# Attention probabilities scaled by GpSimd, and the copies of their transposes shared out anew

## The chip, the cores and the metric

The kernel runs on one core of a Trainium2 chip. Everything is fp32. The metric is the device time of one execution in microseconds (us), taken over whole executions of the program; the profile's span is the time from the first to the last instruction of one profiled execution.

The engines in this text: TensorE (PE; its weight loads are listed apart as PEld), VectorE (DVE), ScalarE (ACT), GpSimd (POOL) and SyncE (SP), which issues most of the loads. A "handoff" is the time between the end of an instruction on one engine and the start of the one that waited for it on another.

## The reference

Two transformer-like blocks of two layers each run over 256 tokens of width 1024. The first block is token mixing by three recurrences with SwiGLU layers, and it is the larger part of the time. The second block has an attention layer, which the change touches, then an HGRN layer, each followed by a SwiGLU layer. The attention:

```python
def gqa_attend(q, k, v):
    s = jnp.einsum('bkgqd,bksd->bkgqs', q, k, preferred_element_type=jnp.float32) * (HEAD_DIM ** -0.5)
    p = jax.nn.softmax(s, axis=-1).astype(v.dtype)
    return jnp.einsum('bkgqs,bksd->bkgqd', p, v)
...
    k_all = jnp.concatenate([k_c, k_l], axis=2)
    v_all = jnp.concatenate([v_c, v_l], axis=2)
    ...  # 256 latent queries, in blocks of 128, against all 512 keys
    o_c = gqa_attend(queries(h_ctx), k_c, v_c)   # 256 context queries against the 256 context keys
```

There are 16 query heads of width 64 and 4 key/value heads.

## The kernel before

The program is written out by hand, one instruction stream for each engine, with semaphores between them. No scheduler orders anything: each engine runs its list from top to bottom, and `wait_ge` holds it until a count is reached.

The attention works in 24 units (`attention_units`). A unit takes two heads (a pair `i`) at a time. The first 16 are **long units** (stream 0, `s == 0`): 128 latent queries against 512 keys, so two score tiles of 128x512. The last 8 are **short units** (stream 1): 256 context queries against 256 keys, so four score tiles of 128x256. Both kinds fill two PSUM banks with scores. For each unit `u`:

1. TensorE computes the scores into one of two pairs of banks (`scores`, `score_pair`).
2. VectorE takes the row maxima and makes the bias from them (`maxes`, L3709 and L3712).
3. ScalarE writes the exponentials into `Pb[:, u % 2]`, with the row sums as a by-product (`exps`, L3599).
4. VectorE inverts the sums (L3719) and multiplies the probabilities by them in place (`scale`, L3723); the last of these raises `probs_scaled`.
5. TensorE turns (transposes) the probabilities, eight tiles of 128x128, into the two banks of `turn_pair` (`turn_probs`, L463).
6. The two banks are copied to `PT` in SBUF (`keep_PT`; L3611 on ScalarE, L3731 on VectorE); each copy raises `PT_ready`. In long units ScalarE copies both banks, in short ones ScalarE copies the first and VectorE the second.
7. TensorE multiplies the values by the turned probabilities (`weigh`), and the result is copied out (`keep_o`; L3737 on VectorE for stream 0, L3618 on ScalarE for stream 1).

The units are pipelined by the loops that call these functions. In step `u` of its loop TensorE does `scores(u)`, `turn_probs(u - 2)` and `weigh(u - 3)`, in this order. `scores(u)` waits for `scores_read` of unit `u - 2`, and `turn_probs(v)` waits for `probs_scaled` of `v` and for both `PT_ready` of the unit before. VectorE does `maxes(u)`, `scale(u - 1)`, `keep_PT(u - 2)`, `keep_o`; ScalarE does `keep_PT(u - 2)`, `exps(u)`, `keep_o`. Recorded matmuls and loads stand at the lines of two helpers: L460 for products, L463 for turnings.

GpSimd has nothing to do in the attention. Its list goes from small loads ahead of it (L4612, L4614) to the wait for `lnp_free` and a load (L4616) long behind it.

Of the kernel before, what the change touches and what calls it, by code (L numbers as in the profile page):

```python
# [20 lines left out]
ALU = mybir.AluOpType  # L21
AX = mybir.AxisListType

P = 128
D = 1024
# [101 lines left out]
def two_blocks(nc, a, out):  # L127
    ctx = ExitStack()
    with ctx:
# [53 lines left out]
        expL_ready = sem("expL_ready")  # L183
        final_norm_landed = sem("final_norm_landed")
        forget_ready = sem("forget_ready")
# [36 lines left out]
        oT_ready = sem("oT_ready")  # L222
        out_norm_landed = sem("out_norm_landed")
        p_T_ready = sem("p_T_ready")
# [36 lines left out]
        std_ready = sem("std_ready")  # L261
        sw_ready = sem("sw_ready")
        v_tok_ready = sem("v_tok_ready")
        var_ready = sem("var_ready")
# [3273 lines left out]
        def act_attention(act):  # L3538
# [69 lines left out]
            def keep_PT(u):  # L3608
                for par in range(2 if units[u][1] == 0 else 1):
                    act.wait_ge(probs_turned, 2 * u + par + 1)  # L3610
                    ins = e.copy(PT[:, u % 4, par], turn_pair[:, par])  # L3611
                    ins.then_inc(act_step, act.up(act_step))
                    act.wait_ge(act_step, act.sent(act_step))
                    act.sem_inc(PT_ready, act.up(PT_ready))
# [7 lines left out]
            for u in range(len(units) + 4):  # L3622
                if 2 <= u < len(units) + 2:
                    keep_PT(u - 2)
                if u < len(units):
                    exps(u)
                if u >= 4 and units[u - 4][1]:
                    keep_o(units[u - 4][0])

        def dve_attention(dve):  # L3630
# [84 lines left out]

            def scale(u):
                r = by_query(u, am[:, 24:32])
                dve.wait_ge(probs_ready, dve.due(probs_ready))
                v.reciprocal(r, by_query(u, am[:, 8:16])).then_inc(dve_step, dve.up(dve_step))  # L3719
                dve.wait_ge(dve_step, dve.sent(dve_step))  # L3720
                n = 2 if units[u][1] == 0 else 4
                for j in range(n):
                    ins = v.tensor_scalar(probs(u, j), probs(u, j), r[:, j:j + 1], None, ALU.mult)  # L3723
                    done = probs_scaled if j == n - 1 else dve_step
                    ins.then_inc(done, dve.up(done))
                dve.wait_ge(dve_step, dve.sent(dve_step))
                dve.wait_ge(probs_scaled, dve.sent(probs_scaled))

            def keep_PT(u):
                dve.wait_ge(probs_turned, 2 * u + 2)  # L3730
                v.tensor_copy(PT[:, u % 4, 1], turn_pair[:, 1]).then_inc(dve_step, dve.up(dve_step))  # L3731
                dve.wait_ge(dve_step, dve.sent(dve_step))
                dve.sem_inc(PT_ready, dve.up(PT_ready))  # L3733

# [6 lines left out]
            for u in range(len(units) + 4):  # L3741
                if u < len(units):
                    maxes(u)
                if 1 <= u <= len(units):
                    scale(u - 1)
                if u >= 2 and u - 2 < len(units) and units[u - 2][1]:
                    keep_PT(u - 2)
                if u >= 4:
                    i, s, qt = units[u - 4]
                    if s == 0 and qt:  # L3750
                        keep_o(i)
# [682 lines left out]
        def pool_hgrn(pool):  # L4434
            e = pool.e
            pool.wait_ge(gb_ready, ends_out[-1])
            for back in range(2):
                pool.wait_ge(gE_ready, queries_exp[back])
                e.tensor_tensor(hF[back], hF[back], hq, ALU.mult).then_inc(pool_product, pool.up(pool_product))
            pool.wait_ge(out_norm_landed, pool.due(out_norm_landed, 16))  # L4440
            pool.wait_ge(hgrn_in_ready, gates_open[0])
# [106 lines left out]
        def second_dve(dve):  # L4548
# [10 lines left out]
            dve_x_sums(dve)  # L4559
            dve.wait_ge(final_norm_landed, dve.due(final_norm_landed, 16))  # L4560
            dve_ffn7(dve, ffn_gated_residual(dve, gtmp7, final=True),
# [15 lines left out]
        def pool_final_weights(pool):  # L4577

            pool.wait_ge(final_norm_landed, pool.due(final_norm_landed, 16))
            for tt in range(2):  # L4580
# [27 lines left out]
        def second_pool(pool):  # L4608
            e = pool.e
            pool.wait_ge(ln_used, pool.due(ln_used))  # L4610
            for j, n in enumerate(("attn_q_norm_2", "attn_k_norm_2")):
                e.dma_start(qkn[:, j], a[n][0:1, :].broadcast_to([P, 64])).then_inc(qk_norm_landed, 16)  # L4612
            pool.wait_ge(ln_cols_used, pool.due(ln_cols_used))
            e.dma_start(cst[:, LVL0:LVL0 + 3 * P], a["cst"][:, LVL0:LVL0 + 3 * P]).then_inc(lvl_landed, 16)  # L4614
            pool.wait_ge(lnp_free, pool.due(lnp_free))
            e.dma_start(lnp[:, 1], a["hgrn_out_norm_2"][0:1, :].broadcast_to([P, D])).then_inc(out_norm_landed, 16)  # L4616
            pool_hgrn(pool)
            e.dma_start(lnp[:, 1], a["final_norm_w_2"].rearrange("(a n) -> a n", a=1).broadcast_to([P, D])
                        ).then_inc(final_norm_landed, 16)
            pool_final_weights(pool)  # L4620
# [164 lines left out]
```

## Time and profile before

| | us |
|---|---|
| Time, median of 3 runs | 3075.56 |
| lowest and highest | 3074.17, 3078.39 |
| Profiled execution: its span | 3075.3 |
| PE busy | 2984.1 (97%) |
| PEld busy | 2376.8 (77%) |
| DVE busy | 1734.7 (56%) |
| ACT busy | 715.3 (23%) |
| POOL busy | 77.7 (3%) |

The profile gives no time for the profiled execution beside its span. The granted TensorE clock is full over the whole span (mean 0.998). Shares of the whole span say little about the change: the 24 attention units lie between about 1990 and 2076 us, less than 3% of the span, and in them VectorE and ScalarE are busy nearly as long as TensorE. A timeline row reads: start in us, duration in us, engine, line, operation, output and inputs, shape, number of instructions merged into the row, and in brackets the idle time of the engine just before, with what ended it.

### The profile page before, as it was taken

The page shows a single profiled execution, that of the slowest core. Times are in us where ns is not written, and L with a number is a line of the kernel's source. Part 1 is how long each engine was busy: PE and PEld are TensorE (multiplying, and loading weights), DVE is VectorE, ACT ScalarE, POOL GpSimd, SP SyncE. Part 2 cuts the span into 40 slices and gives each one's busy share as a digit, 9 for nine tenths or more (in the row PEclk, how much of TensorE's full clock was granted, in tenths as well). Part 3 has the DMA queues.
Part 4 walks back from the last instruction along what each step waited for, and adds up shares of the span by engine and source line. Part 5 has one row for each costly group of instructions (what it writes and reads, how often), then busy time and mean ns, then how long its engine had stood idle before and what let it go on. Part 6 is the DMA issues. An engine that isn't in the chain of part 4 may idle for free. (4 is left out here: it accounts for less than half of the span.)

```text
span 3075.3 us, 53460 instructions
## 1 busy us (share of the span) xinstructions
PE 2984.1 (97%) x23086; PEld 2376.8 (77%) x23086; DVE 1734.7 (56%) x2567; ACT 715.3 (23%) x1371; POOL 77.7 (3%) x105
## 2 busy tenths in 40 slices
PE   8999999999999999999999999989999999999998
PEld 8988775559987998685558985655888887766897
DVE  5554456446556564464546556584333664486666
ACT  2102114222112101223322104282111012254210
POOL 1000000000001000000000000000000000001000
PEclk9999999999999999999999999999999999999999
DMA  8645403237656746313227744102222443231553
GB/s 288 223 175 184 142 30 110 97 110 234 206 183 196 260 164 216 134 60 108 99 83 234 237 141 151 55 1 83 82 82 83 150 154 113 98 122 63 165 165 110
DMA packets 279818, 429.94 MB, mean 140 GB/s; under 512 B 10072, under 2 KB 147776, under 8 KB 279584
## 3 DMA queue, kind: packets, MB, share of 16 engines
q1 hardware_dynamic: 273936, 411.52, 39.5%
q0 software_dynamic: 5024, 13.82, 1.4%
q8 instruction: 183, 3.00, 0.4%
q10 hardware_dynamic: 624, 1.19, 0.1%
q14 instruction: 51, 0.42, 0.0%
HBM read 425.45 MB, written 1.05 MB: 139 GB/s over the span
## 5 line engine op out<-in xcount | busy, mean ns | idle before, releaser
L460 PE MATMUL bank<-arena 64*64 64x64 f32 (+8 forms) x7292 | 740.9, 281 | 23.3 <-DVE arena L2069 4.6
L460 PE MATMUL bank<-xT,ring 128*128 128x128 f32 (+2 forms) x4512 | 725.1, 320 | 10.3 <-DVE arena L852 5.7
L460 PEld LDWEIGHTS bank<-arena 128*128 128x128 f32 (+3 forms) x7292 | 640.6, 161 | 120.1 <-issue 36.6
L460 PEld LDWEIGHTS bank<-xT,ring 128*128 128x128 f32 (+1 forms) x4512 | 657.7, 191 | 71.2 <-issue 10.5
L460 PE MATMUL bank<-ring,xT 128*128 128x512 f32 (+3 forms) x1648 | 577.2, 519 | 2.2 <-DVEq L2086 1.2
L460 PEld LDWEIGHTS bank<-ring,xT 128*128 128x128 f32 (+1 forms) x1648 | 264.0, 182 | 253.5 <-issue 237.0
L460 PE MATMUL bank<-ring,arena 128*128 128x256 f32 (+1 forms) x1584 | 436.9, 427 | 12.4 <-issue 5.3
L460 PEld LDWEIGHTS bank<-ring,arena 128*128 128x128 f32 x1584 | 298.2, 190 | 123.9 <-issue 82.0
L852 DVE TENSOR_TENSOR arena<-arena,bank 128x256 f32<-128x256 f32 (+1 forms) x198 | 92.2, 466 | 395.7 <-PE bank L460 254.7
L763 ACT COPY arena<-bank 128x256 f32<-128x256 f32 (+1 forms) x264 | 107.7, 408 | 747.2 <-PE bank L460 745.9
L812 DVE TENSOR_TENSOR arena<-ring,arena 128x1024 f32<-128x1024 f32 (+1 forms) x216 | 257.1, 1190 | 7.4
L812 DVE TENSOR_TENSOR arena<-ring 128x1024 f32<-128x1024 f32 (+1 forms) x108 | 129.6, 1200 | 89.6 <-PE bank L460 84.7
L460 PE MATMUL bank<-arena,ring 128*128 128x128 f32 (+1 forms) x1152 | 168.2, 300 | 0.0
L460 PEld LDWEIGHTS bank<-arena,ring 128*128 128x128 f32 x1152 | 154.4, 192 | 7.0
L460 PE MATMUL bank<-xT,arena 128*128 128x128 f32 (+1 forms) x1104 | 157.9, 296 | 0.0
L460 PEld LDWEIGHTS bank<-xT,arena 128*128 128x128 f32 x1104 | 145.2, 192 | 5.8
L812 DVE TENSOR_TENSOR ring<-ring 128x1024 f32<-128x1024 f32 (+1 forms) x108 | 128.6, 1191 | 3.7
L463 PEld LDWEIGHTS bank<-cst,arena 128*128 128x128 f32 x482 | 54.0, 141 | 38.0 <-DVE arena L3723 22.2
L793 ACT COPY arena<-bank 128x256 f32<-128x256 f32 x14 | 5.2, 373 | 324.7 <-PE bank L460 324.7
L463 PE MATMUL bank<-cst,arena 128*128 128x128 f32 x482 | 66.9, 276 | 11.4 <-DVEq L3733 6.3
L906 DVE TENSOR_TENSOR arena<-arena,bank 128x256 f32<-128x256 f32 x56 | 23.6, 421 | 78.2 <-PE bank L460 77.1
L841 DVE TENSOR_TENSOR arena<-arena 128x512 f32<-128x512 f32 (+1 forms) x66 | 51.6, 781 | 25.6 <-ACT arena L782 21.1
(421 smaller groups left out, 2186.8 us busy)
## 6 DMA issues: line engine op xcount, KB each, us to landing
ring<-in_ffn_w SPq DMA_DIRECT2D x88, 1024.0 KB, 8.0
ring<-in_w_in SPq DMA_DIRECT2D x32, 2048.0 KB, 7.7
ring<-in_ffn_w_in SPq DMA_DIRECT2D x44, 1024.0 KB, 6.5
arena<-in_ada_w SPq DMA_DIRECT2D x20, 2048.0 KB, 13.2
ring<-in_ffn_w SPq DMA_DIRECT2D x16, 2048.0 KB, 7.9
ring<-in_ffn_w_out SPq DMA_DIRECT2D x12, 2048.0 KB, 7.8
ring<-in_hgrn_w_in SPq DMA_DIRECT2D x12, 2048.0 KB, 7.9
ring<-in_ffn_w SPq DMA_DIRECT2D x8, 1536.0 KB, 6.6
```

Source lines behind the costliest of these rows:

```text
L460: return self.e.matmul(o, lhsT, rhs, start=start, stop=stop, skip_group_check=True)
L463: return self.e.transpose(o, x, ident[0:n, 0:n])
L763: ins = e.copy(w.s[:, i], bank[:, 0:w.T])
L793: e.copy(w.kept[:, 0], banks[0][:, 0:256]).then_inc(down_kept, act.up(down_kept))
L812: v.tensor_tensor(out_, a_, b_, ALU.subtract).then_inc(T_sums, dve.up(T_sums))
L841: ins = v.tensor_tensor(w.hid_block(b), c4[:, :, :, 0], c4[:, :, :, 1], ALU.mult)
L852: ins = v.tensor_tensor(out_, kept, c, ALU.add)
L906: v.tensor_tensor(out_, a_, b_, ALU.add).then_inc(done, dve.up(done))
```

## The change

It does three things in the attention, and one that only renames.

- The inversion of the row sums stays on VectorE, in a function `invert`, and raises a new semaphore, `sums_inverted`. The multiplications go to GpSimd, in a new function `pool_attention`, called between the two loads named above. It has one wait for `sums_inverted` per unit and a wait for its own completion behind each of its multiplications: 32 of 128x512 and 32 of 128x256.
- In long units ScalarE copies the first bank of the turned probabilities and VectorE the second.
- In short units VectorE copies both, and ScalarE none.
- `final_norm_landed` and `out_norm_landed` become one semaphore, `lnp_row_landed`, with counts 16 and 32.

```diff
@@ act_attention
             def keep_PT(u):
-                for par in range(2 if units[u][1] == 0 else 1):
-                    act.wait_ge(probs_turned, 2 * u + par + 1)
-                    ins = e.copy(PT[:, u % 4, par], turn_pair[:, par])
+                if units[u][1] == 0:
+                    act.wait_ge(probs_turned, 2 * u + 1)
+                    ins = e.copy(PT[:, u % 4, 0], turn_pair[:, 0])
                     ins.then_inc(act_step, act.up(act_step))
                     act.wait_ge(act_step, act.sent(act_step))
                     act.sem_inc(PT_ready, act.up(PT_ready))
@@
+        def pool_attention(pool):
+            e = pool.e
+            for u in range(len(attention_units())):
+                r = by_query(u, am[:, 24:32])
+                pool.wait_ge(sums_inverted, u + 1)
+                n = 2 if units_stream(u) == 0 else 4
+                for j in range(n):
+                    ins = e.tensor_scalar(probs(u, j), probs(u, j), r[:, j:j + 1], None, ALU.mult)
+                    done = probs_scaled if j == n - 1 else pool_step
+                    ins.then_inc(done, pool.up(done))
+                    pool.wait_ge(done, pool.sent(done))
@@ dve_attention
-            def scale(u):
-                r = by_query(u, am[:, 24:32])
+            def invert(u):
                 dve.wait_ge(probs_ready, dve.due(probs_ready))
-                v.reciprocal(r, by_query(u, am[:, 8:16])).then_inc(dve_step, dve.up(dve_step))
-                dve.wait_ge(dve_step, dve.sent(dve_step))
-                n = 2 if units[u][1] == 0 else 4
-                for j in range(n):
-                    ins = v.tensor_scalar(probs(u, j), probs(u, j), r[:, j:j + 1], None, ALU.mult)
-                    done = probs_scaled if j == n - 1 else dve_step
-                    ins.then_inc(done, dve.up(done))
-                dve.wait_ge(dve_step, dve.sent(dve_step))
-                dve.wait_ge(probs_scaled, dve.sent(probs_scaled))
+                ins = v.reciprocal(by_query(u, am[:, 24:32]), by_query(u, am[:, 8:16]))
+                ins.then_inc(sums_inverted, dve.up(sums_inverted))
+                dve.wait_ge(sums_inverted, dve.sent(sums_inverted))
 
             def keep_PT(u):
-                dve.wait_ge(probs_turned, 2 * u + 2)
-                v.tensor_copy(PT[:, u % 4, 1], turn_pair[:, 1]).then_inc(dve_step, dve.up(dve_step))
-                dve.wait_ge(dve_step, dve.sent(dve_step))
-                dve.sem_inc(PT_ready, dve.up(PT_ready))
+                for par in (1,) if units[u][1] == 0 else range(2):
+                    dve.wait_ge(probs_turned, 2 * u + par + 1)
+                    v.tensor_copy(PT[:, u % 4, par], turn_pair[:, par]).then_inc(dve_step, dve.up(dve_step))
+                    dve.wait_ge(dve_step, dve.sent(dve_step))
+                    dve.sem_inc(PT_ready, dve.up(PT_ready))
@@ loop of dve_attention
                 if 1 <= u <= len(units):
-                    scale(u - 1)
-                if u >= 2 and u - 2 < len(units) and units[u - 2][1]:
+                    invert(u - 1)
+                if 2 <= u < len(units) + 2:
                     keep_PT(u - 2)
@@ second_pool
+            pool_attention(pool)
             pool.wait_ge(lnp_free, pool.due(lnp_free))
```

On VectorE, two long units in a row of the program before (`bank` is PSUM, `arena` is SBUF; L3723 is the scaling, L3737 the copy of a finished head pair):

```order
L3709 TENSOR_REDUCE arena<-bank 128x2
L3712 TENSOR_SCALAR arena<-arena 128x2
L3719 RECIPROCAL arena<-arena 128x2
L3723 TENSOR_SCALAR arena<-arena 128x512 x2
L3709 TENSOR_REDUCE arena<-bank 128x2
L3712 TENSOR_SCALAR arena<-arena 128x2
L3719 RECIPROCAL arena<-arena 128x2
L3723 TENSOR_SCALAR arena<-arena 128x512 x2
L3737 COPY arena<-bank 128x256
```

The same place of the changed program (its lines stand some 11 lower; here L3737 is the copy of a turned bank and L3743 that of a finished pair):

```order
L3721 TENSOR_REDUCE arena<-bank 128x2
L3724 TENSOR_SCALAR arena<-arena 128x2
L3730 RECIPROCAL arena<-arena 128x2
L3737 COPY arena<-bank 128x512
L3721 TENSOR_REDUCE arena<-bank 128x2
L3724 TENSOR_SCALAR arena<-arena 128x2
L3730 RECIPROCAL arena<-arena 128x2
L3737 COPY arena<-bank 128x512
L3743 COPY arena<-bank 128x256
```

Two scalings from SBUF have gone from each long unit, and one copy from PSUM has come.

On VectorE, two short units in a row before:

```order
L3709 TENSOR_REDUCE arena<-bank 128x4
L3712 TENSOR_SCALAR arena<-arena 128x4
L3719 RECIPROCAL arena<-arena 128x4
L3723 TENSOR_SCALAR arena<-arena 128x256 x4
L3731 COPY arena<-bank 128x512
L3709 TENSOR_REDUCE arena<-bank 128x4
L3712 TENSOR_SCALAR arena<-arena 128x4
L3719 RECIPROCAL arena<-arena 128x4
L3723 TENSOR_SCALAR arena<-arena 128x256 x4
L3731 COPY arena<-bank 128x512
```

And now:

```order
L3721 TENSOR_REDUCE arena<-bank 128x4
L3724 TENSOR_SCALAR arena<-arena 128x4
L3730 RECIPROCAL arena<-arena 128x4
L3737 COPY arena<-bank 128x512 x2
L3721 TENSOR_REDUCE arena<-bank 128x4
L3724 TENSOR_SCALAR arena<-arena 128x4
L3730 RECIPROCAL arena<-arena 128x4
L3737 COPY arena<-bank 128x512 x2
```

Four scalings have gone from each short unit, and a second copy has come. TensorE's list is the same before and now.

## Rows read from the trace of the kernel before

**Rows 1.** Busy time by engine, turnings 2 to 9, seven units (PE, PEld, DVE, ACT, POOL).
```profile
2000.88:2022.62 21.74, 21.74 (x198) 14.07 (x196) 18.38 (x38) 18.55 (x42) 0.00 (x0) 1.00 0.01 2
```

**Rows 2.** Timeline, one long unit on TensorE and VectorE.
```profile
2014.33 2.15 PE L460 MATMUL bank<-arena 128*64 128x128 f32 x20
...
2016.62 1.22 DVE L3709 TENSOR_REDUCE arena<-bank 128x2 f32<-128x1024 f32 x1 [0.57 <-PE bank L460]
...
2018.29 0.88 DVE L3723 TENSOR_SCALAR arena<-arena 128x512 f32<-128x512 f32 x2
...
2019.52 1.09 PE L463 MATMUL bank<-cst,arena 128*128 128x128 f32 x8
```

**Rows 3.** Timeline, the first exponential of two long units on ScalarE.
```profile
2009.88 0.69 ACT L3599 ACTIVATE arena<-bank,arena 128x512 f32<-128x512 f32 x1 [0.20 <-ACT arena L3611]
...
2013.07 0.69 ACT L3599 ACTIVATE arena<-bank,arena 128x512 f32<-128x512 f32 x1 [0.20 <-ACT arena L3611]
```

**Rows 4.** Timeline of TensorE, turnings 1 and 15.
```profile
1997.77 1.09 PE L463 MATMUL bank<-cst,arena 128*128 128x128 f32 x8 [0.67 <-DVE arena L3723]
...
2041.74 1.07 PE L463 MATMUL bank<-cst,arena 128*128 128x128 f32 x8
```

**Rows 5.** Timeline, one short unit on VectorE and TensorE.
```profile
2062.19 1.23 DVE L3709 TENSOR_REDUCE arena<-bank 128x4 f32<-128x1024 f32 x1
2062.25 1.06 PE L463 MATMUL bank<-cst,arena 128*128 128x128 f32 x8 [0.60 <-DVEq L3733]
...
2063.24 2.15 PE L460 MATMUL bank<-arena 128*64 128x256 f32 x16
...
2063.87 1.14 DVE L3723 TENSOR_SCALAR arena<-arena 128x256 f32<-128x256 f32 x4
...
2065.10 0.69 DVE L3731 COPY arena<-bank 128x512 f32<-128x512 f32 x1
...
2065.94 1.23 DVE L3709 TENSOR_REDUCE arena<-bank 128x4 f32<-128x1024 f32 x1
```

**Rows 6.** Timeline, the last turnings (22 and 23) and the last copy.
```profile
2069.74 1.06 PE L463 MATMUL bank<-cst,arena 128*128 128x128 f32 x8 [1.67 <-DVEq L3733]
...
2072.28 1.06 PE L463 MATMUL bank<-cst,arena 128*128 128x128 f32 x8 [0.46 <-DVEq L3733]
...
2073.39 0.69 DVE L3731 COPY arena<-bank 128x512 f32<-128x512 f32 x1 [1.31 <-PE bank L463]
```

**Rows 7.** Timeline, GpSimd beside VectorE and ScalarE in the first block.
```profile
517.25 2.53 DVE L2387 TENSOR_TENSOR arena<-arena 128x256 f32<-128x256 f32 x4
...
519.86 1.10 POOL L2327 TENSOR_TENSOR arena<-arena 128x512 f32<-128x512 f32 x1 [0.36 <-DVE arena L2387]
...
521.05 0.42 ACT L2300 ACTIVATE arena<-arena 128x256 f32<-128x256 f32 x1 [0.59 <-POOL arena L2327]
...
581.28 1.27 POOL L2545 TENSOR_TENSOR arena<-arena 128x512 f32<-128x512 f32 x1 [56.54 <-ACT arena L2575]
582.62 2.27 POOL L2545 TENSOR_TENSOR arena<-arena,cst 128x512 f32<-128x512 f32 x2
```

**Rows 8.** Timeline of GpSimd, its other kinds and sizes.
```profile
0.24 0.10 POOL L4776 MEMSET const-float32-0.0<- 128x1 f32 x1 [0.24 <-issue]
...
31.46 0.20 POOL L1217 MEMSET rows<- 128x128 f32 x1 [10.16 <-ACTq L3132]
...
2808.53 4.67 POOL L4445 TENSOR_TENSOR xT<-xT,lnp 128x1024 f32<-128x1024 f32 x2 [10.12 <-ACTq L4238]
...
3031.71 1.26 POOL L4583 TENSOR_TENSOR xtok<-xtok,lnp 128x512 f32<-128x512 f32 x1 [217.64 <-DVEq L3352]
```

**Rows 9.** Timeline of VectorE around GpSimd's last row above.
```profile
3029.35 0.69 DVE L3339 TENSOR_TENSOR arena<-arena,lnp 128x512 f32<-128x512 f32 x1
...
3031.64 0.42 DVE L906 TENSOR_TENSOR arena<-arena,bank 128x256 f32<-128x256 f32 x1
3032.10 1.42 DVE L3339 TENSOR_TENSOR arena<-arena,lnp 128x512 f32<-128x512 f32 x1
```

More of the change, by code:

```diff
@@ L183, in two_blocks @@
         expL_ready = sem("expL_ready")
-        final_norm_landed = sem("final_norm_landed")
         forget_ready = sem("forget_ready")
@@ L222, in two_blocks @@
         oT_ready = sem("oT_ready")
-        out_norm_landed = sem("out_norm_landed")
+        lnp_row_landed = sem("lnp_row_landed")
         p_T_ready = sem("p_T_ready")
@@ L262, in two_blocks @@
         sw_ready = sem("sw_ready")
+        sums_inverted = sem("sums_inverted")
         v_tok_ready = sem("v_tok_ready")
@@ L4439, in pool_hgrn @@
                 e.tensor_tensor(hF[back], hF[back], hq, ALU.mult).then_inc(pool_product, pool.up(pool_product))
-            pool.wait_ge(out_norm_landed, pool.due(out_norm_landed, 16))
+            pool.wait_ge(lnp_row_landed, pool.due(lnp_row_landed, 16))
             pool.wait_ge(hgrn_in_ready, gates_open[0])
@@ L4559, in second_dve @@
             dve_x_sums(dve)
-            dve.wait_ge(final_norm_landed, dve.due(final_norm_landed, 16))
+            dve.wait_ge(lnp_row_landed, dve.due(lnp_row_landed, 32))
             dve_ffn7(dve, ffn_gated_residual(dve, gtmp7, final=True),
@@ L4577, in pool_final_weights @@
         def pool_final_weights(pool):
-            pool.wait_ge(final_norm_landed, pool.due(final_norm_landed, 16))
+            pool.wait_ge(lnp_row_landed, pool.due(lnp_row_landed, 16))
             for tt in range(2):
@@ L4614, in second_pool @@
             e.dma_start(cst[:, LVL0:LVL0 + 3 * P], a["cst"][:, LVL0:LVL0 + 3 * P]).then_inc(lvl_landed, 16)
+            pool_attention(pool)
             pool.wait_ge(lnp_free, pool.due(lnp_free))
-            e.dma_start(lnp[:, 1], a["hgrn_out_norm_2"][0:1, :].broadcast_to([P, D])).then_inc(out_norm_landed, 16)
+            e.dma_start(lnp[:, 1], a["hgrn_out_norm_2"][0:1, :].broadcast_to([P, D])).then_inc(lnp_row_landed, 16)
             pool_hgrn(pool)
             e.dma_start(lnp[:, 1], a["final_norm_w_2"].rearrange("(a n) -> a n", a=1).broadcast_to([P, D])
-                        ).then_inc(final_norm_landed, 16)
+                        ).then_inc(lnp_row_landed, 16)
             pool_final_weights(pool)
```

## Prediction

> **What bounds the kernel now.** I read the page first: TensorE is busy for 97% of the span at full clock. So a change on other engines can cost time wherever TensorE waits for them, and can win only what TensorE waits for now. Then I read the timeline of the attention, where alone the change acts, and followed one unit through the engines.
>
> In long units TensorE works without a pause at first: seven units take 21.74 us, and it is busy for 21.74 of them [rows 1]. That is 3.106 us per unit, and no change on other engines makes it less. ScalarE, with both copies, needs 3.19 (2009.88 to 2013.07) [rows 3] and falls behind, until later TensorE follows its pace. The 14 steps from turning 1 to turning 15 take 43.97 us [rows 4] where TensorE alone would need 43.48. So only 0.5 us can be won there.
>
> In short units VectorE is the bound: from one maximum to the next 3.75 us pass (2062.19 to 2065.94), filled by maximum, bias and inverse, 1.68 until the scaling starts, then four scalings in 1.14 and a copy that with its gap takes 0.84 (2065.10 to 2065.94). TensorE needs only 0.99 (the turning, 2062.25 to 2063.24) + 2.15 = 3.14 [rows 5]. From turning 15 to turning 22 the 7 steps take 28.00 us, 4.00 each, as ScalarE's backlog falls into the first of them [rows 4, 6].
>
> **The change, part by part.** Let p be the time of one GpSimd scaling of 128x512, and q that of one of 128x256. Neither is in the trace.
>
> *The loop that the change makes longer.* The scaling used to lie on VectorE between the inverse and the turning. Now it lies there on GpSimd. In step u TensorE does the scores of u, turns u-2, weighs u-3. VectorE inverts unit u-1 behind the maximum of u, and GpSimd can start on u-1 only then. So there is a ring: scores of u, maximum of u, inverse of u-1, GpSimd on u-1, turning of u-1 (in step u+1), weighing, scores of u+2. It spans two units; each microsecond by which it is too long costs half a microsecond per unit.
>
> *Long units.* The inverse ends at 2018.26 (0.03 before the scaling at 2018.29), the turning of this unit starts at 2019.52 [rows 2]: a window of 1.26 us. Before, the scaling filled 0.88 of it. Now it must hold a handoff from VectorE to GpSimd (0.08: 517.25 + 2.53 = 519.78, start 519.86), two scalings, the wait for its own completion between them (0.07: two of 1.10 in 2.27) and a handoff on (0.09: 520.96 to 521.05) [rows 7]; handoff to TensorE taken as that to ScalarE. The turning is late by d = 2p + 0.24 - 1.26 = 2p - 1.02, if that is positive. Over 14 steps: 43.48 + 7d - 43.97 = 14p - 7.63.
>
> *Short units.* The same ring, for two units: TensorE's end to VectorE's start 0.14 (2016.48 to 2016.62 [rows 2]), maximum to end of inverse 1.65, GpSimd 0.08 + 4q + 3 x 0.07 + 0.09 = 4q + 0.38, turning 0.99, weighing and scores 2.15 [rows 5]. Sum 5.31 + 4q. Over 7 steps: 3.5 x (5.31 + 4q) - 28.00 = 14q - 9.42. VectorE's own work is now 1.68 + 2 x 0.84 = 3.36 per unit, a floor of the step; it binds while q is below 0.35.
>
> *Off the path.* ScalarE loses 24 copies. In long units it had 3.19 of work against TensorE's 3.106 and loses one of two copies; in short ones VectorE set the step, and ScalarE loses its only copy. So it is late in neither; its backlog at turning 15 goes, and that gain is in the 28.00 above. VectorE's copy in long units (0.84) takes the place of scalings (0.88), so its load stays. The wait in `keep_PT` holds the next maximum behind it on VectorE; the bank is half turned by then and the copy starts within the turning, so the ring above stays the longer one. GpSimd's list has only the wait for `lnp_free`, hundreds of microseconds later, behind the new work: nothing. The renamed semaphore: nothing.
>
> *End.* The last short unit has two copies in a row on VectorE. Before, the copy starts at 2073.39; now the second starts after half a turning (0.53), 0.05 and 0.84: 2073.70, 0.3 late [rows 6]. For GpSimd's longer work before turning 23 I allow another 0.2 (an estimate). Together +0.5.
>
> *Sum:* 14p - 7.63 + 14q - 9.42 + 0.5 = 14 (p + q) - 16.55.
>
> **The two unknown prices.** From below: a MEMSET only writes, 0.10 us for one element per partition and 0.20 for 128 [rows 8], so 0.8 ns per element, and p = 0.50, q = 0.30. From above: a TENSOR_TENSOR reads two tensors and writes one, 1.26 us for 512 and 4.67 / 2 = 2.34 for 1024 [rows 8], so 2.1 ns per element, and p = 1.26, q = 0.72. A scaling reads one and writes one. It has one stream more than the first and one less than the second, so I take the middle: p = 0.88, q = 0.51. Then the sum is 14 x 1.39 - 16.55 = +2.9 us: long units +4.7 (half of 2p - 1.02 = 0.74 in each, 3.48 per step), short units -2.3 (3.67 per step), end +0.5. On the profiled span, 3075.3 + 2.9 = 3078.2; the median of the runs is 0.3 above that span, so 3078.5.
>
> Two ops of GpSimd of 512 elements show 1.26 and 1.10 us here [rows 7, 8], and no single-input one is in the trace. The Trainium skill, GPSIMD Engine Reference, section Elementwise — side-by-side cycle accounting, gives a measured 769 ns for 512 elements as its best case. An estimate from that page is p = 0.77 and q = 0.38, by which the sum would be 14 x 1.15 - 16.55 = -0.4, so 3075.1; it would still be no change that can be told.
>
> **The rivals.**
>
> *GpSimd is fast (p near 0.50).* For it: a scaling need not share its reads with a second tensor, and MEMSET goes at 0.8 ns. Against it: reads and writes may share time as the two reads seem to. Then d is nothing, the long part is -0.5, and short steps are held by VectorE's 3.36: 7 x 3.36 - 28.00 = -4.5. With the end +0.5: -4.5, or 3071.1. Even that is less than 0.2%.
>
> *GpSimd is as slow as with two inputs (p = 1.26, q = 0.72).* This is the one on the other side. Place: the same ring, each second turning waits 1.5 us. Price 14 x 1.98 - 16.55 = +11.2, or 3086.8. It counts as slower (by over 0.2%, 6.2 us, about what a measurement of this kernel can tell from no change) from p + q = 1.62, which on the line between the two bounds is p = 1.03. For it: the arithmetic of GpSimd in these rows runs near that rate. Against it: all of it has two inputs.
>
> *VectorE and GpSimd hold each other up.* The trace shows it: beside GpSimd's TENSOR_TENSOR (3031.71 to 3032.97), VectorE's operation with two inputs in SBUF took 1.42 us where the same took 0.69 before. But an operation that had one of its inputs in PSUM, and was running when GpSimd started, took its usual 0.42 [rows 9]. In the attention VectorE's long operations (maximum, copies) read PSUM alone, so I cost this at nothing. If the copies of the turned banks, which start just behind the inverse and so beside GpSimd, were held for one scaling each, VectorE would need 1.68 + 0.84 + 0.88 = 3.40 in a long unit, still under 3.48, but 3.36 + 2 x 0.51 = 4.38 in a short one against 3.67 (+5.0 over 7). With the sum above +7.9: 3083.5.
> The Trainium skill, SBUF — State Buffer, section Who interferes with whom, says that VectorE in a two-port mode and GpSimd block each other for a whole instruction, and that a VectorE instruction with at most one SBUF input outside these modes does not contend. The pair of rows on the two VectorE operations agrees; the large SBUF scaling that could contend leaves VectorE with this change, and what is left (bias and inverse, 2 or 4 elements) comes behind two copies and a maximum (0.84 + 0.84 + 1.23 = 2.91 in a short unit), when GpSimd's work on a unit (4q + 0.21 = 2.25) is done.
>
> **How the numbers follow.** Forecast (p between 0.65 and 1.03): 0.54. Fast GpSimd: 0.15. Slow GpSimd (p above 1.03): 0.25. Mutual blocking: 0.06. The first gives -2 to +6, which is within 0.2%; so does nearly all of the second. Faster by over 0.2% needs -6.2 us, more than the sum of all floors wins: 0.03, for what I have overlooked. Slower: of the last two cases nearly all, 0.29, less a little for the part of them that stays under the bound: 0.28. Same: 0.69. The range goes from the fast case, 3071.5, to the slow one at its full price, 3087; beyond them I leave about 0.15 together.
>
> **What would show it.** GpSimd scalings of about 0.88 and 0.51 us. Turnings in long units alternate: one step near 3.1, the next near 3.85, with TensorE waiting for GpSimd in each second step. Short steps near 3.7, where TensorE waits for GpSimd too, and VectorE idles a little. No wait of TensorE for ScalarE's exponentials at the change from long to short. VectorE's copies at 0.69 though GpSimd runs beside them. I am wrong if TensorE waits for something other than GpSimd in most steps, if maxima or copies are longer than before, or if GpSimd's gaps are much over 0.1 us.

## The result, and the profile after

| | before | changed |
|---|---|---|
| Time, median of 6 runs (us) | 3076.36 | 3102.57 |
| lowest and highest | 3073.87, 3078.39 | 3100.80, 3121.43 |
| ratio of the times | | 1.0096, 95% interval 1.0086 to 1.0106 |
| Span of the profiled execution | 3075.3 | 3100.5 |
| POOL busy | 77.7 | 157.1 |

By the medians the change costs 26 us (0.85%). The ratio of 0.96% comes out higher, since the one execution of 3121.43 counts in it; its mean granted clock was 0.990, that of the others 0.995 to 0.997. Either way the time lies clearly outside the predicted range of 3071.5 to 3087. The profiled execution's own time was 3102.53. The forecast was a small loss of 2.9 us; a loss it is, but nine times as large.

All of it arises in the attention. The page shows the engines over 40 slices of the span; look at slice 27 of DVE, ACT and POOL. The kernel before:

```profile
DVE  5554456446556564464546556584333664486666
ACT  2102114222112101223322104282111012254210
POOL 1000000000001000000000000000000000001000
```

The changed kernel:

```profile
PE   8999999999999999999999999979999999999998
DVE  5554556446646555455446556554433564486666
ACT  2102114221112102213221113352111011255210
POOL 1000000000001000000000000270000000001000
```

TensorE's first product of attention scores began at 1989.10 before and begins at 1985.58 in this execution; the first product behind the attention began at 2075.88 and begins at 2101.24. So the attention takes 115.66 us in place of 86.78, 28.9 more. The 3.5 us by which it begins earlier are not the change's doing: over all the kernels of this text that have the attention, whose programs ahead of it differ by a small instruction or two at most, it begins between 1985.58 and 1991.13. What comes behind takes as long as it did (999.4 and 999.3 us).

One long unit in the timeline of the changed kernel (L3637 is GpSimd's scaling):

```profile
2041.08 1.09 PE L463 MATMUL bank<-cst,arena 128*128 128x128 f32 x8 [0.63 <-POOL arena L3637]
2042.10 2.15 PE L460 MATMUL bank<-arena 128*64 128x128 f32 x20
...
2042.29 3.22 POOL L3637 TENSOR_SCALAR arena<-arena 128x512 f32<-128x512 f32 x2 [1.27 <-DVE arena L3730]
...
2044.37 1.22 DVE L3721 TENSOR_REDUCE arena<-bank 128x2 f32<-128x1024 f32 x1 [0.83 <-PE bank L460]
2045.57 1.09 PE L463 MATMUL bank<-cst,arena 128*128 128x128 f32 x8 [1.31 <-POOL arena L3637]
...
2045.83 0.17 DVE L3730 RECIPROCAL arena<-arena 128x2 f32<-128x2 f32 x1
2046.16 3.23 POOL L3637 TENSOR_SCALAR arena<-arena 128x512 f32<-128x512 f32 x2 [0.65 <-DVE arena L3730]
...
2049.44 1.09 PE L463 MATMUL bank<-cst,arena 128*128 128x128 f32 x8 [0.70 <-POOL arena L3637]
```

This answers to [rows 2]. There the window from the inverse to the turning was 1.26 us; here two scalings alone take 3.22, and each turning waits for GpSimd, which ends at 2045.51 and 2049.39. TensorE waits for VectorE only once more, for 0.23 us at the last weighing. Its waits for GpSimd in the attention, in the changed kernel (total us, times, longest):

```profile
PE bank L463 <- POOL arena L3637: 28.5, 20, 3.8
```

The prices, from the groups of instructions between 1990 and 2101 us (count, busy us, mean ns):

```profile
L3637 POOL TENSOR_SCALAR arena<-arena 128x512 f32<-128x512 f32 x32 | 50.0, 1563 | 104.3 <-DVE arena L3730 102.6
...
L3637 POOL TENSOR_SCALAR arena<-arena 128x256 f32<-128x256 f32 x32 | 29.5, 922 | 9.9 <-DVE arena L3730 7.4
L3737 DVE COPY arena<-bank 128x512 f32<-128x512 f32 x32 | 22.1, 692 | 20.2 <-PE bank L463 18.5
```

So p = 1.56 and q = 0.92, where the prediction took 0.88 and 0.51 and held 1.26 and 0.72 for the upper ends. VectorE's copies stay at 0.69 us.

There is a second thing that the prediction did not have: TensorE's clock. Its two levels are 1.2 GHz, shown as 0.50, and 2.4 GHz, shown as 1.00. Busy time and granted clock by stretches in the changed kernel (PE, PEld, DVE, ACT, POOL, then the clock):

```profile
1995.00:1997.00 2.00, 2.00 (x8) 0.76 (x6) 0.69 (x1) 1.70 (x4) 1.85 (x2) 0.50 0.00 0
1997.00:2003.00 6.00, 3.99 (x34) 2.46 (x33) 3.81 (x7) 2.42 (x7) 3.53 (x3) 0.99 0.00 0
2003.00:2007.20 4.20, 4.20 (x26) 2.20 (x24) 0.69 (x1) 2.14 (x5) 2.72 (x2) 0.61 0.00 0
2007.20:2035.00 27.80, 21.39 (x196) 14.06 (x196) 17.67 (x32) 14.21 (x33) 19.75 (x13) 1.00 0.01 2
...
2071.00:2076.60 5.60, 4.62 (x24) 2.88 (x24) 2.47 (x5) 2.56 (x9) 4.61 (x5) 0.70 0.01 3
2076.60:2082.00 5.40, 3.26 (x26) 2.03 (x24) 4.54 (x8) 2.70 (x10) 3.10 (x4) 1.00 0.00 2
2082.00:2087.00 5.00, 4.36 (x24) 3.03 (x24) 1.38 (x2) 2.20 (x8) 4.28 (x5) 0.66 0.01 2
```

From 1995 to 1997 it is at the lower level, and again for parts of later stretches, behind longer waits of TensorE: it had waited 2.18 us before the turning at 1993.68, and 2.78 before that at 2082.64. Such a turning takes 1.97 us where [rows 2] has 1.09. Not every long wait brings it: TensorE also waited 1.97 us before the turning at 2012.39, and the stretch around it is at 1.00. For the whole attention, from its first product to the first one behind it, before and then changed:

```profile
1989.10:2075.88 86.78, 77.98 (x665) 51.40 (x665) 70.04 (x154) 70.93 (x179) 0.00 (x0) 1.00 0.00 1
```
```profile
1985.58:2101.24 115.66, 86.39 (x665) 55.77 (x665) 63.99 (x114) 56.78 (x155) 79.52 (x64) 0.93 0.00 1
```

The same 665 products and turnings keep TensorE busy for 8.4 us longer.

### The profile page after: what moved, and what is told of

It is laid out like the page before. It is cut to its first block, busy times and chain, and to the rows that moved or that the text cites. A ratio compares the mean times of both kernels' runs of the same rounds, so it can differ in the third digit from the quotient of the medians.

```text
span 3100.5 us, 53484 instructions
## 1 busy us (share of the span) xinstructions
PE 2988.7 (96%) x23086; PEld 2381.2 (77%) x23086; DVE 1728.3 (56%) x2527; ACT 700.7 (23%) x1347; POOL 157.1 (5%) x169
## 4 chain that ended last, share of the span: by engine, by line
PE 88%; DVE 7%; ACT 2%; POOL 1%; issue 1%; DMA 0%; DVEq 0%; ACTq 0%; POOLq 0%
PE bank L460 86%; PE bank L463 2%; POOL arena L3637 1%; DVE arena L812 1%; DVE arena L3721 1%; DVE ring L812 0%; ACT xT L1086 0%; DVE arena L906 0%; DVE arena L2069 0%; DMA xtok<-in_x 0%; DVE arena L2081 0%; DVE arena L4409 0%; DVE stats L1001 0%; DVE xT L1108 0%; DVE arena L1903 0%
## 5 line engine op out<-in xcount | busy, mean ns | idle before, releaser
L3637 POOL TENSOR_SCALAR arena<-arena 128x512 f32<-128x512 f32 (+1 forms) x64 | 79.5, 1242 | 114.3 <-DVE arena L3730 110.0
```

Of the source, the lines that this page charges most:

```text
L3637: ins = e.tensor_scalar(probs(u, j), probs(u, j), r[:, j:j + 1], None, ALU.mult)
```

## The experiments

The theory (A): GpSimd's own price, put into the ring between the inverse and the turning, makes the time; each microsecond there costs half a microsecond per unit. Rivals: VectorE beside it makes GpSimd slow (B in e1); the new sharing of the copies costs (B in e2 and e3); the clock adds to it (C) or not (D). To compare stages closely I use one length throughout, from turning 1 to the first product behind the attention, each from its own profile: 78.11 us before (1997.77 to 2075.88), 103.87 changed (1997.37 to 2101.24). I call it the stage. It leaves out the head of the attention, from the first product of scores to turning 1, which takes 8.67 us before and 11.79 changed; where that matters it is said.

**e1: GpSimd's operations alone.** A small kernel of its own, all work of the original left out.

```python
run(lambda: e.tensor_scalar(y[:, 0:w_], y[:, 0:w_], s[:, 0:1], None, ALU.mult))     # L48
run(lambda: e.tensor_scalar(y[:, 0:w_], y[:, 0:w_], 0.5, None, ALU.mult))           # L49
run(lambda: e.tensor_tensor(y[:, 0:w_], y[:, 0:w_], w[:, 0:w_], ALU.mult))          # L50
run(lambda: e.tensor_tensor(y[:, 0:w_], y[:, 0:w_], s[:, 0:1].broadcast_to([P, w_]), ALU.mult))  # L51
```

> This kernel leaves the whole computation out: it only times GpSimd. Sets of four, each waiting for its own completion: multiplication by a per-partition scalar from SBUF, by a constant, by a second tensor, by a broadcast column, at 512 and 256 elements; the first at 1024, and one tensor_tensor of 2x512 by two broadcast columns; then the scaling of 512 beside VectorE maxima out of PSUM, and beside VectorE copies out of PSUM and tiny SBUF scalings. Theory A (the price is GpSimd's own): the scaling of 512 takes 1.5 to 1.6 us with VectorE idle too, 256 takes 0.92, and beside maxima it is the same. Rival B (VectorE beside it makes it slow): 0.6 to 1.1 us alone and 1.5 beside the maxima. The broadcast form of 1024 should take 2.3 by the rows of tensor_tensor, against 2 x 1.56.

Groups of its instructions (L60 and L61 are the scaling of 512 with VectorE busy beside it, L53 the broadcast form of 2x512):

```profile
L60 POOL TENSOR_SCALAR y<-y,s 128x512 f32<-128x512 f32 x8 | 12.5, 1565 | 1.0 <-POOL y L61 0.2 <-POOL y L53 0.2
...
L52 POOL TENSOR_SCALAR y<-y,s 128x1024 f32<-128x1024 f32 x4 | 11.4, 2844 | 0.4
L53 POOL TENSOR_TENSOR y<-y,s 128x1024 f32<-128x1024 f32 x4 | 7.6, 1893 | 0.3
L48 POOL TENSOR_SCALAR y<-y,s 128x512 f32<-128x512 f32 x4 | 6.3, 1564 | 6.8 <-DVEq L87 6.5
L49 POOL TENSOR_SCALAR y<-y 128x512 f32<-128x512 f32 x4 | 6.0, 1490 | 0.3
L50 POOL TENSOR_TENSOR y<-y,w 128x512 f32<-128x512 f32 x4 | 5.0, 1262 | 0.3
L51 POOL TENSOR_TENSOR y<-y,s 128x512 f32<-128x512 f32 x4 | 4.2, 1040 | 0.3
```

A holds, B falls: 1.56 us with VectorE idle and 1.57 beside it. The order of prices is what I had taken as impossible: multiplying by one number per partition (1.56), or by a constant (1.49), is dearer than multiplying by a whole second tensor (1.26), and the same product with the column broadcast as a second tensor costs 1.04. For a whole unit, 1.89 us in this form stand against 2 x 1.56; I had expected 2.3.

**e2: the new sharing of the copies alone.** The scaling is back on VectorE, `pool_attention` gone.

```diff
-                    invert(u - 1)
+                    scale(u - 1)
...
-            pool_attention(pool)
```

> The scaling is back on VectorE, the new sharing of the copies stays. Theory A (the time went into the ring through GpSimd): the 25 us do not come with the copies. But VectorE now has maximum to inverse 1.68, scaling 0.91, copy 0.84 and half of a 0.45 copy = 3.65 in a long unit and 1.68 + 1.17 + 1.68 = 4.5 in a short one, where the kernel before took 3.14 and 4.00: +7 and +4 and a little at the end, 3088 (3084 to 3092). Rival B (the copies are what costs): 3100 or more.

3089.16 us, ratio 1.0044 (1.0029 to 1.0059); the stage takes 91.75. As A expected. TensorE's waits are now for VectorE (long steps, then short steps, TensorE's timeline):

```profile
2014.06 1.07 PE L463 MATMUL bank<-cst,arena 128*128 128x128 f32 x8 [0.33 <-DVEq L3746]
2017.99 1.07 PE L463 MATMUL bank<-cst,arena 128*128 128x128 f32 x8 [0.78 <-DVEq L3746]
...
2070.93 1.06 PE L463 MATMUL bank<-cst,arena 128*128 128x128 f32 x8 [1.44 <-DVEq L3746]
2075.51 1.06 PE L463 MATMUL bank<-cst,arena 128*128 128x128 f32 x8 [1.44 <-DVEq L3746]
```

So the copies could not have moved to VectorE without the scaling moving off it; half of the change alone is a loss too, of another kind.

**e3: GpSimd's scaling alone**, the copies shared as before.

```diff
-                if units[u][1] == 0:
-                    act.wait_ge(probs_turned, 2 * u + 1)
+                for par in range(2 if units[u][1] == 0 else 1):
+                    act.wait_ge(probs_turned, 2 * u + par + 1)
...
-                if 2 <= u < len(units) + 2:
+                if u >= 2 and u - 2 < len(units) and units[u - 2][1]:
                     keep_PT(u - 2)
```

> GpSimd scales, the copies are shared as before the change. Theory A: ScalarE's and VectorE's copies are off the ring, so the time is that of the changed kernel within 3 us: 3102 (3099 to 3106). Rival B (copies): back to 3076 to 3085.

3105.32 us (3097.80 to 3107.40), ratio 1.0086 (1.0069 to 1.0102), within the expectation; the stage takes 103.80 (2002.54 to 2106.34), against 103.87 in the changed kernel. That they agree so closely is partly chance, since the clock fell in other places: its long part is 1.4 shorter and its short part 1.7 longer. Surer are two long steps at full clock:

```profile
2011.36 1.09 PE L463 MATMUL bank<-cst,arena 128*128 128x128 f32 x8 [0.59 <-POOL arena L3637]
...
2019.72 1.09 PE L463 MATMUL bank<-cst,arena 128*128 128x128 f32 x8 [0.59 <-POOL arena L3637]
```

They take 8.36 us, as in the changed kernel (2041.08 to 2049.44). The sharing of the copies changes nothing that can be told once GpSimd is in the ring.

**e4: the clock.** Four turnings of the identity ahead of each wait of TensorE for GpSimd.

```diff
-                pe.wait_ge(probs_scaled, u + 1)
                 if u:
                     pe.wait_ge(PT_ready, 2 * u)
+                for _ in range(4):
+                    pe.turn(turn_pair[:, 0, 0:P], ident)
+                pe.wait_ge(probs_scaled, u + 1)
```

> The changed kernel with four turnings of the identity, which compute nothing, before TensorE waits for GpSimd in each unit; they take about 0.5 us of a wait of 0.4 to 2.8. The changed kernel has TensorE at its lower clock level in four stretches of the attention, and it is 4.8 us longer busy there. Theory C (the waits bring the lower level, and it adds some 3 us to the 22 of the ring): with TensorE busier the stretches go, 3098 to 3100. Rival D (the lower level costs nothing since TensorE waits anyway): 3102 to 3104.

3098.02 us (3096.64 to 3099.42) against 3102.57 (3100.80 to 3121.43): 4.5 less, though TensorE has more to do. The ratios to the kernel before are 1.0070 (1.0055 to 1.0085) and 1.0096 (1.0086 to 1.0106). The two were measured at different times and the intervals all but touch, so the profiles have to bear it out: the stage takes 98.19 (1998.90 to 2097.09), 5.7 less, and the whole attention (1987.49 to 2097.09) 109.60, 6.1 less. The clock over the attention and some 2.5 us ahead of it:

```profile
1985.00:2097.10 112.10, 95.05 (x780) 63.32 (x778) 64.25 (x115) 57.83 (x158) 79.52 (x64) 1.00 0.00 1
```

The clock is full throughout. C holds, and the clock's part is 4.5 us by the times and about 6 by the profiles, more than the 3 that I expected. The 4.8 us of longer busy time in the expectation were too low as well; counted over the same instructions they are 8.4. Without idle turnings the time goes with the mean clock in the same way: e3 took 3097.80 us in its one execution at 0.998, and 3105.13 to 3107.40 at 0.995.

**e7: half of GpSimd's work**, the test of the prediction's own sum. Half of the probabilities stay unscaled.

```diff
-                n = 2 if units_stream(u) == 0 else 4
+                n = 1 if units_stream(u) == 0 else 2
```

> The changed kernel, but only half of each unit's probabilities are scaled (work left out: one scaling of 512 in long units, two of 256 in short ones). GpSimd's work is 1.56 and 1.94 us, as if p were 0.74 and q 0.43. The sum of the prediction, 14 (p + q) - 16.55, gives -0.2, so 3076; with the measured handoffs +1, 3077. If the ring is wrong and the copies or the semaphores cost something by themselves, the time stays above 3085.

3077.02 us, ratio 1.0001 (0.9992 to 1.0011); the stage takes 78.12 (1997.66 to 2075.78), as before, and the head 0.8 more. The sum gave -0.2 for the stage. In its timeline of TensorE, long steps alternate between 3.11 and 3.60:

```profile
2024.42 1.09 PE L463 MATMUL bank<-cst,arena 128*128 128x128 f32 x8 [0.42 <-POOL arena L3637]
2027.53 1.09 PE L463 MATMUL bank<-cst,arena 128*128 128x128 f32 x8
2031.13 1.09 PE L463 MATMUL bank<-cst,arena 128*128 128x128 f32 x8 [0.42 <-POOL arena L3637]
```

With the formula d is 2 x 0.74 - 1.02 = 0.46, and 3.106 + 0.46 = 3.57 for every second step. The ring is as it was described; what was put into it was wrong.

**e5: the cheaper form.** One `tensor_tensor` per unit.

```diff
-                for j in range(n):
-                    ins = e.tensor_scalar(probs(u, j), probs(u, j), r[:, j:j + 1], None, ALU.mult)
+                x = Pb[:, u % 2].rearrange("p r n -> p (r n)").rearrange("p (q n) -> p q n", q=n)
+                ins = e.tensor_tensor(x, x, r.unsqueeze(2).broadcast_to([P, n, 1024 // n]), ALU.mult)
...
```

> GpSimd scales a whole unit by one tensor_tensor with the inverses broadcast, 1.89 us alone, where the changed kernel needs 3.22 in a long and 3.97 in a short unit. Theory A (each microsecond of GpSimd's work costs half a microsecond per unit): 0.16 + 1.89 + 0.05 against the window of 1.26 gives d = 0.84 and 3.106 + 0.42 per long step, +5.4 over 14; the short ring 0.14 + 1.65 + 2.10 + 3.14 = 7.03 for two units, 3.51 per step, -3.4 over 7; in all +2 to +4, TensorE mostly at the higher clock level: 3079. Rival E (GpSimd on the path costs by being another engine, whatever it takes): over 3090.

3080.38 us, ratio 1.0012 (1.0004 to 1.0021), stage 80.04. Every second long turning waits, as the ring has it:

```profile
2027.77 1.09 PE L463 MATMUL bank<-cst,arena 128*128 128x128 f32 x8 [0.73 <-POOL arena L3637]
...
2030.88 1.09 PE L463 MATMUL bank<-cst,arena 128*128 128x128 f32 x8
```

As A says and not E: 22 of the 26 us go with the form of the instruction, the engine being the same. They include what the lower clock had cost, for the clock is full here.

**e6: GpSimd also makes the inverses**, to leave the ring through VectorE's next maximum. The scaling is that of e5, and VectorE's `invert` is gone.

```diff
-                pool.wait_ge(sums_inverted, u + 1)
+                pool.wait_ge(probs_ready, u + 1)
+                e.tensor_tensor(r, by_query(u, am[:, 8:16]), small[:, 63:64].broadcast_to([P, r.shape[1]]), ALU.pow)
...
```

> As e5_one_broadcast, and GpSimd makes the inverses itself (a tensor_tensor with pow -1 on 2 or 4 columns), so it can start as soon as the exponentials are done and not behind VectorE's next maximum. Theory A: the ring then spans three units (0.14 + maximum 1.44 + exponentials 1.7 + GpSimd 2.3 to 2.9 + 4.2 for turning, weighing and scores, some 10 us for three), below TensorE's 3.106 in long units and near 3.3 in short ones: 3072 to 3076, at or below the kernel before, if the pow takes under 0.5 us; up to 3077 if it takes 1. Rival F (not the place in the ring but GpSimd's time per unit counts): as e5 or slower, 3079 to 3084.

3081.79 us, ratio 1.0021 (1.0013 to 1.0030), stage 83.91. The pow of 2 columns takes 0.70 us and that of 4 takes 1.01, for which A allowed at most 3077, so A missed; the time lies in the 3079 to 3084 of rival F. But GpSimd's time per unit is not the reason, as e9 will show. Timeline:

```profile
2020.82 1.22 DVE L3724 TENSOR_REDUCE arena<-bank 128x2 f32<-128x1024 f32 x1 [0.60 <-PE bank L460]
...
2022.04 1.89 POOL L3641 TENSOR_TENSOR arena<-arena 128x1024 f32<-128x1024 f32 x1
2022.08 1.88 DVE L3727 TENSOR_SCALAR arena<-arena 128x2 f32<-128x2 f32 x1
...
2024.08 0.69 ACT L3599 ACTIVATE arena<-bank,arena 128x512 f32<-128x512 f32 x1 [1.56 <-DVE arena L3727]
...
2026.09 0.17 DVE L3727 TENSOR_SCALAR arena<-arena 128x2 f32<-128x2 f32 x1
```

VectorE's multiplication of two columns, 0.17 us as a rule, began 0.04 behind GpSimd's operation and ended 0.03 behind its end. ScalarE waits for it with the exponentials, every second long unit. In the other long units, as at 2026.09, it falls beside GpSimd's pow of 2 columns and is not held. This is the mutual blocking that the prediction had as a rival, on an instruction that it had excused. It led to e9.

**e8: GpSimd in short units only**, by the form of e5, with long units as before.

```diff
-            for u in range(len(attention_units())):
+            for u in range(16, len(attention_units())):
...
```

> Long units as in the kernel before (VectorE scales, ScalarE copies both banks); in short units GpSimd scales by the broadcast form and VectorE copies both banks. Theory A: long part 0, short part: about 3.5 per step in place of 3.75, less a longer first step, -1 to -3: 3073 to 3075. If the copies of short units on VectorE or the handoff are dearer than thought: 3078 or more.

3075.30 us, ratio 0.9996 (0.9988 to 1.0005), just above the expected 3073 to 3075; stage 76.65, 1.5 shorter, as expected. That is too little for the time of the whole to tell.

**e9 to e12: VectorE's small multiplication away.** The factor -0.125 goes once into the norm weights of the queries; the same edit on four kernels (e6, the one before, e8, e5).

```diff
+            v.tensor_scalar(qkn[:, 0], qkn[:, 0], -0.125, None, ALU.mult).then_inc(dve_step, dve.up(dve_step))
...
-                    ins = v.tensor_reduce(top[:, q_], src[:, q_] if u == 0 else src, AX.X, ALU.max)
...
-                    ins = v.tensor_scalar(bias[:, q_], top[:, q_], -0.125, None, ALU.mult)
+                    ins = v.tensor_reduce(bias[:, q_], src[:, q_] if u == 0 else src, AX.X, ALU.min)
...
-                    ins = e.activation(probs(u, j), src, ACT.Exp, scale=0.125, bias=bias[:, j:j + 1],
+                    ins = e.activation(probs(u, j), src, ACT.Exp, scale=-1.0, bias=bias[:, j:j + 1],
```

> e6_gpsimd_inverts, with VectorE's little multiplication (the bias) taken away: -0.125 is folded into the weights of the queries' norm once, the maximum becomes a minimum and ScalarE's scale -1. In e6 this multiplication of 2 columns lasts 1.88 us in every second long unit, for just as long as GpSimd's operation beside it, and 0.17 otherwise. Theory G (the two engines' shared way to SBUF holds VectorE up, and that is why e6 missed its forecast): long steps go from 3.66 to 3.11 and short ones to 3.4, 3072 (3071 to 3074). Rival H (e6 is slow since GpSimd now has 2.8 us of work per unit, with 0.70 us for two columns of pow): within 2 us of e6 less 0.2 per unit, 3077 to 3080.

> The kernel before with the same folding and nothing on GpSimd. VectorE is the bound only in short units: 3.75 less 0.20 there, nothing in long ones: -1.6 to -2.5, 3074.

> e8_short_units_only with the folding. The short ring loses 0.20 of 7.03: 0.1 per step, -1 against e8: 3074.

> e5_one_broadcast with the folding. GpSimd's work did not meet the bias there, so theory G and the ring both give only the 0.20 that leaves the ring, 0.1 per step or -2.3: 3078.

| | us | ratio to before | stage | the same with the multiplication |
|---|---|---|---|---|
| e9 | 3073.97 | 0.9993 (0.9984 to 1.0002) | 75.31 | e6: 3081.79, 83.91 |
| e10 | 3075.74 | 0.9999 (0.9990 to 1.0008) | 77.68 | before: 78.11 |
| e11 | 3075.12 | 0.9998 (0.9989 to 1.0007) | 76.35 | e8: 3075.30, 76.65 |
| e12 | 3076.56 | 1.0002 (0.9993 to 1.0012) | 77.88 | e5: 3080.38, 80.04 |

In e9 the long steps are TensorE's own again (timeline of TensorE, nothing in brackets):

```profile
2021.04 1.09 PE L463 MATMUL bank<-cst,arena 128*128 128x128 f32 x8
2024.14 1.09 PE L463 MATMUL bank<-cst,arena 128*128 128x128 f32 x8
```

G holds: the edit is worth 8.6 us of the stage where the blocking was, and 0.3 to 2.2 where it was not. H, which gave 3077 to 3080, falls, and with it F, as GpSimd does the same work in e9 as in e6. e9 has the shortest stage of all, 2.8 us under the kernel before (2.1 with the head counted in: 84.68 against 86.78), but its interval holds 1: no version here is shown to beat the kernel before. e12 came out as expected by the stage (2.2 for 2.3). e10 gained 0.4 where at least 1.6 was expected, and e11 0.3 where it was 1. In e10 the short steps that VectorE bounds are 0.2 shorter, as expected (3.54 for 3.75), but this reaches only five of the seven steps, while the long part is 0.2 and the end 0.4 longer.

## Why the prediction was wrong

The attention has four parts: the head, from the first product of scores to turning 1; the 14 steps from turning 1 to turning 15; the 7 steps from there to turning 22; and the end, from there to the first product behind. The prediction had a term for each of the last three and none for the head. What each part gained or lost against the kernel before, read from TensorE's timelines, and in brackets what the prediction's terms give with GpSimd's measured times (for e5, what its expectation gave):

| us | head | turnings 1 to 15 | 15 to 22 | end |
|---|---|---|---|---|
| kernel before, its length | 8.67 | 43.97 | 28.00 | 6.14 |
| changed | +3.1 | +16.5 (+14.3) | +7.4 (+3.5) | +1.9 (+0.5) |
| e4, the same at full clock | +2.7 | +14.5 (+14.3) | +3.7 (+3.5) | +1.9 (+0.5) |
| e7, half of the work | +0.8 | +2.9 (+2.7) | -3.4 (-3.4) | +0.5 (+0.5) |
| e5, the cheaper form | +1.1 | +5.1 (+5.4) | -3.5 (-3.4) | +0.4 |

- *What bounds the kernel, and where.* Right. Everything outside the attention stayed as it was, TensorE's waits decide, and the floors were those named: 3.11 per long step in e9, and in e5, e7 and e8 no short step under 3.34, where 3.36 was named.
- *The ring and its price of 14 us per microsecond of p and of q.* Right, shown part by part by e7, e5 and e4. With the measured p = 1.563 and q = 0.922 the long part is 14 x 1.563 - 7.63 = +14.3 and the short one 14 x 0.922 - 9.42 = +3.5; with +0.5 at the end that is 18.3 of the 28.9 us by which the attention is longer. One sign of it was forecast too simply: both long turnings of a pair are late in the changed kernel (waits of 1.31 and 0.70), not only each second one. The pair takes 8.36 us, as the ring has it (2 x 3.106 + 2 x 1.563 - 1.02 = 8.32). In e7 and e5 the pattern is the predicted one.
- *The failed step: "From above: a TENSOR_TENSOR reads two tensors and writes one, 1.26 us for 512".* It took the operation with more streams for a bound on the one with fewer. Measured (e1, VectorE idle): 1.56 with one tensor, 1.26 with two. The middle value 0.88 was 0.68 too low, and 0.51 for q was 0.41 too low: 14 x (0.68 + 0.41) = 15.3 us. The range, cut off at this false bound, missed the time for the same reason. The estimate worked out from the best case of 769 ns in the Trainium skill, GPSIMD Engine Reference, section Elementwise — side-by-side cycle accounting, was further off still. Why GpSimd's `tensor_scalar` is the slower form is not shown.
- *TensorE's clock was left out.* TensorE's waits grew to 2 us and more, and the clock fell behind several of them. The changed kernel less e4 puts this at 6.1 us of the attention, 3.7 of them in the steps from turning 15 to 22; the times put it at about 4.5. In e5, e7 and e9, with waits of at most 1.3 us, the attention's granted clock stays at 1.00. It does not take GpSimd: in e2, where TensorE waits for VectorE, it falls to 0.79 over the last 8 us, behind a wait of 2.50 us.
- *The end and the head.* The end came 1.9 us later and not 0.5. Between the last two turnings 4.06 us pass (2.54 before), as GpSimd's four scalings of the last unit stand alone between them; the allowance for this was 0.2. The two copies in a row make the remaining 0.4, where 0.3 was expected. The head had no term and took 3.1 more, 2.7 at full clock, for GpSimd's first scalings. The handoffs were not those assumed either: VectorE to GpSimd took 0.16 us (2046.00 to 2046.16) and not 0.08, GpSimd to TensorE 0.06 (2045.51 to 2045.57) and not 0.09; this is small beside the rest, as the two middle parts of e4 are each within 0.2 of the terms.
- *Together.* The prices 15.3, the clock 6.1, the end 1.4, the head 2.7 and 0.4 in the steps make 25.9; with the forecast of 2.9 that is 28.8 of the measured 28.9. Each part is from one profile of each kernel.
- *The rivals.* The slow case was the right one in kind, at chance 0.25, and too cheap. The lower end of the range, 3071.5, is 0.4 above the fast case's own 3071.1; nothing hangs on it. Mutual blocking was real but played next to no part in this kernel: VectorE's multiplication of the maxima was held up only twice (0.56 and 0.41, against 0.17). The reason given for its harmlessness, that it comes when GpSimd is done, mostly held here although GpSimd was slow, because in this kernel GpSimd starts only behind VectorE's inverse. In e6, where GpSimd no longer waits for VectorE, it did not hold, and the blocking shows its full price.
- *ScalarE off the path.* Right: TensorE never waits for it in the attention.

## What to carry to other kernels

An operation that the trace does not show has no upper bound in a neighbour that looks harder: a two-tensor instruction on GpSimd did not bound the one-tensor one. Where a change hangs on one such price and the slope is 14 to 1, time the instruction by itself first, in the forms that would do. Add what the longer waits do to TensorE's clock, and the first and last units, where the pipeline hides nothing. And ask what ring a moved step lies in and how many units it spans: the slack of the slot between its neighbours (here 1.26 us) is what it may cost, not the idle time of the engine that it goes to.

## What the runs showed of the hardware

- GpSimd's `tensor_scalar` in fp32: 0.92, 1.56 and 2.84 us for 256, 512 and 1024 elements, 2.5 ns for each further element; with a constant 1.49 for 512. `tensor_tensor` on two tensors: 0.72 and 1.26 for 256 and 512; with a broadcast column 0.61, 1.04, and 1.89 for 2x512. A `pow` on 2 columns took 0.70 and on 4 columns 1.01.
- A VectorE `tensor_scalar` of 2 columns in SBUF was held for the whole of a GpSimd `tensor_tensor` of 1024 (1.88 us in place of 0.17, e6). Beside GpSimd's `tensor_scalar` it was held at times, until that instruction's end (0.56 and 0.41 us in the changed kernel), and at other times not at all. In e1 it was held once in five times, and then not to the end of GpSimd's instruction. What decides this is open. Beside GpSimd's `pow` of 2 columns it was not held (0.17, e6). The Trainium skill, SBUF — State Buffer, section Who interferes with whom, states such blocking for VectorE's two-port modes and as lasting the whole instruction. If this small multiplication is in such a mode, which no run shows, the holds in e6 agree and the free passes in e1 do not. Maxima and copies out of PSUM were never longer beside GpSimd (1.23 and 0.69).
- TensorE's granted clock was 0.93 over the attention in the changed kernel, whose waits reach 3.84 us, and 1.00 in e4, where 0.66 us of idle turnings stand in each and the longest pause left is 1.58 us. The lower level made the same 665 instructions 8.4 us longer (77.98 and 86.39).
